# Scaling attention's projection weights on GpSimd ahead of its block sums, in a two-layer decoder step

## The reference, cut to what matters

```python
def rms_norm(x, gain):
    xf = x.astype(jnp.float32)
    xf = xf * lax.rsqrt(jnp.mean(xf * xf, axis=-1, keepdims=True) + RMS_EPS)
    return (xf * gain.astype(jnp.float32)).astype(x.dtype)

def shared_kv(h, norm_kv, w_kv, k_norm, w_fgate, b_fgate):
    u = rms_norm(h, norm_kv)
    k, v = jnp.split(u @ w_kv, 2, axis=-1)
    ...
def fox_layer(x, norm_g, w_in, q_norm, w_o, k_all, v_all, c_all):
    q, gate = jnp.split(rms_norm(x, norm_g) @ w_in, 2, axis=-1)
    q = rms_norm(q.reshape(bsz, t, B_HEADS, B_DH), q_norm)
    o = forgetting_attention(q, k_all, v_all, c_all)
    o = o.reshape(bsz, t, B_WIDTH).astype(x.dtype) * jax.nn.silu(gate)
    return x + o @ w_o, ...
```

## Time and profile before

| | |
|---|---|
| median of 3 runs | 1575.26 us |
| lowest and highest run | 1572.15 and 1576.94 us |
| span of the profiled execution, first to last instruction | 1572.7 us |
| mean granted TensorE clock | 0.995 |
| TensorE busy | 1529.1 us, 97% |
| VectorE busy | 1010.7 us, 64% |
| ScalarE busy | 713.1 us, 45% |
| GpSimd busy | 434.0 us, 28% |
| multiplications by the norms' factors, L457, on VectorE | 32, 1.22 us each |
| GpSimd's idle time ahead of the key multiplications, L845 | 226.5 us |
| GpSimd's idle time ahead of the first block sum, L708 | 257.0 us |

### The profile page before, as it was taken

The page is one execution under the profiler, slowest core; times in us unless marked ns, Lnnn a source line. Parts: engine busy times, 40 slices in busy tenths (PEclk is TensorE's granted clock), DMA queues, the critical chain, the costliest instruction groups (busy, mean ns, idle before and its releaser), DMA issues.

```text
span 1572.7 us, 23771 instructions
## 1 busy us (share of the span) xinstructions
PE 1529.1 (97%) x8705; PEld 1135.8 (72%) x8705; DVE 1010.7 (64%) x1979; ACT 713.1 (45%) x1412; POOL 434.0 (28%) x336
## 2 busy tenths in 40 slices
PE   6999999999999999999999999999999999998997
PEld 4688888888888874446777777777777777764543
DVE  7478696877869684135465776767676767676311
ACT  4344455544445552121365555555465555545100
POOL 6012222121222101012243425343343425332200
PEclk9999999999999999999999999999999999999999
DMA  9663929466482943223233545364444445475231
GB/s 267 175 191 120 265 73 269 123 188 194 130 246 89 271 174 84 78 87 100 82 95 107 161 161 175 135 199 137 156 137 142 157 161 175 148 235 216 89 131 42
DMA packets 254085, 242.32 MB, mean 154 GB/s; under 512 B 23162, under 2 KB 219962, under 8 KB 253970
## 3 DMA queue, kind: packets, MB, share of 16 engines
q1 hardware_dynamic: 242834, 204.21, 42.5%
q0 software_dynamic: 11136, 36.59, 6.6%
HBM read 212.63 MB, written 95.24 MB: 196 GB/s over the span
## 4 chain that ended last, share of the span: by engine, by line
PE 90%; DVE 5%; ACT 3%; issue 2%; DMA 0%; SPq 0%; POOL 0%; DVEq 0%; ACTq 0%; POOLq 0%
PE psum L1987 46%; PE psum L2011 7%; PE psum L2496 7%; PE psum L2294 5%; PE psum L2317 4%; PE psum L2301 3%; PE psum L2064 3%; PE psum L2256 2%; PE psum L2350 2%; PE psum L1975 2%; PE psum L2134 1%; PE psum L2150 1%; PE psum L2075 1%; PE psum L2162 1%; PE psum L2152 1%
## 5 line engine op out<-in xcount | busy, mean ns | idle before, releaser
L1987 PE MATMUL psum<-arena 128*128 128x252 f32 (+1 forms) x3472 | 815.2, 385 | 4.5 <-ACT arena L921 3.9
L1987 PEld LDWEIGHTS psum<-arena 128*128 128x128 f32 x3472 | 643.1, 191 | 125.8 <-issue 30.5
L1339 DVE TENSOR_TENSOR arena<-arena,psum 128x252 f32<-128x252 f32 (+1 forms) x310 | 130.6, 421 | 205.0 <-PE psum L1987 195.9
L845 POOL TENSOR_TENSOR arena<-arena 128x1024 f32<-128x1024 f32 x64 | 160.7, 2511 | 226.5 <-DMA arena<-k_pages 208.6
L1157 ACT ACTIVATE arena<-psum,arena 128x256 f32<-128x256 f32 (+7 forms) x128 | 93.7, 739 | 117.0 <-DVE arena L1684 116.7
L921 ACT COPY arena<-psum 128x252 f32<-128x252 f32 (+1 forms) x124 | 45.9, 370 | 172.3 <-PE psum L1987 172.2
L2496 PE MATMUL psum<-arena 128*128 128x512 f32 x256 | 114.4, 597 | 0.0
L2011 PE MATMUL psum<-arena 128*128 128x512 f32 x256 | 113.1, 594 | 0.1
L708 POOL TENSOR_TENSOR arena<-arena 128x512 f32<-128x512 f32 x31 | 40.9, 1319 | 257.0 <-issue 127.0
L1166 ACT ACTIVATE arena<-arena 128x256 f32<-128x256 f32 (+7 forms) x128 | 92.4, 770 | 2.1
L2011 PEld LDWEIGHTS psum<-arena 128*128 128x128 f32 x256 | 47.5, 190 | 57.5 <-issue 56.5
(11 more groups left out here) (265 smaller groups left out, 2150.8 us busy)
## 6 DMA issues: line engine op xcount, KB each, us to landing
k_pages<-in_cache_k SPq DMA_DIRECT2D x64, 512.0 KB, 6.5
v_pages<-in_cache_v SPq DMA_DIRECT2D x64, 512.0 KB, 7.2
arena<-k_pages SPq DMA_DIRECT2D x64, 512.0 KB, 3.6
arena<-v_pages SPq DMA_DIRECT2D x64, 512.0 KB, 5.7
arena<-in_w_in_a SPq DMA_DIRECT2D x32, 512.0 KB, 6.9
arena<-in_x_prompt SPq DMA_DIRECT2D x16, 512.0 KB, 5.5
arena<-in_w_kv SPq DMA_DIRECT2D x16, 512.0 KB, 5.6
arena<-in_w_in_b SPq DMA_DIRECT2D x16, 512.0 KB, 7.3
```

The source lines that it names most:

```text
L845: pool.tensor_tensor(k_ring[:, m % 2], k_ring[:, m % 2], q_all[:, m % S:m % S + 1, :].broadcast_to([P, PAGES, P]), ALU.mult).then_inc(kq_m ...
L1339: dve.tensor_tensor(out, more, bank[n % 2][:, 0:size(u)], ALU.add).then_inc(of.by_dve, 1)
L1987: ins = pe.matmul(bank[n % 2][:, 0:size(u)], w[:, k, :], x[:, k, :], start=(k == 0 and r in (0, 1, 3, 4)), stop=(k == HK - 1), skip_group_ ...
```

## The change

`scale_w` is issued by GpSimd instead of VectorE. Each call leaves its place in VectorE's list, and two calls stand at the head of `sums_of_kq` and of `sums_of_vg`. The waits for the loads move with them; GpSimd then waits for its own scalings before the sums. One wait is added, ahead of the first K and Q scaling, for the loads of the factors.

```diff
-        def scale_w(dve, w, gain, p, loaded, scaled):
-
-            dve.wait_ge(loaded, 16 * (p + 1))
-            dve.tensor_tensor(w, w, gain.unsqueeze(2).broadcast_to([P, KT, P]), ALU.mult).then_inc(scaled, 1)
+        def scale_w(pool, w, gain, p, loaded, scaled):
+
+            pool.wait_ge(loaded, 16 * (p + 1))
+            pool.tensor_tensor(w, w, gain.unsqueeze(2).broadcast_to([P, KT, P]), ALU.mult).then_inc(scaled, 1)
...
             def sums_of_kq(q):
+                scale_w(pool, w_k, gain_kv, q, w_k_loaded, w_k_scaled)
+                scale_w(pool, w_q, gain_b, q, w_q_loaded, w_q_scaled)
                 pool.wait_ge(w_k_scaled, q + 1)
                 pool.wait_ge(w_q_scaled, q + 1)
...
             def sums_of_vg(p):
+                scale_w(pool, w_v, gain_kv, p, w_v_loaded, w_v_scaled)
+                scale_w(pool, w_g, gain_b, p, w_g_loaded, w_g_scaled)
                 pool.wait_ge(w_v_scaled, p + 1)
                 pool.wait_ge(w_g_scaled, p + 1)
...
                 if s == TT - 3:
+                    pool.wait_ge(keys_in, 16 * 10)
                     sums_of_kq(0)
...
             me.chain(dve.tensor_scalar(gain_q2, gain_q2, -(DH ** -0.5), None, ALU.mult))
-            scale_w(dve, w_k, gain_kv, 0, w_k_loaded, w_k_scaled)
-            scale_w(dve, w_q, gain_b, 0, w_q_loaded, w_q_scaled)
             tile(5)
             tile(6)
-            scale_w(dve, w_v, gain_kv, 0, w_v_loaded, w_v_scaled)
-            scale_w(dve, w_g, gain_b, 0, w_g_loaded, w_g_scaled)
             tile(TT - 1)
...
             vg_add(0, 8)
-            scale_w(dve, w_k, gain_kv, 1, w_k_loaded, w_k_scaled)
             new_score(0)
...
                 vg_add(p, 10)
-                if p == 0:
-                    scale_w(dve, w_q, gain_b, 1, w_q_loaded, w_q_scaled)
                 row_max(p, 1)
...
                 kq(5)
-                if nxt:
-                    scale_w(dve, w_v, gain_kv, p + 1, w_v_loaded, w_v_scaled)
                 row_max(p, 4)
...
                 kq(8)
-                if nxt:
-                    scale_w(dve, w_g, gain_b, p + 1, w_g_loaded, w_g_scaled)
                 row_max(p, 5)
...
                 vg(3)
-                if p + 2 < PAIRS:
-                    scale_w(dve, w_k, gain_kv, p + 2, w_k_loaded, w_k_scaled)
                 row_max(p, 7)
...
                     new_score(p + 1)
-                if p + 2 < PAIRS:
-                    scale_w(dve, w_q, gain_b, p + 2, w_q_loaded, w_q_scaled)
```

## The result

| | before | after |
|---|---|---|
| median | 1574.65 us (4 runs, 1572.15 to 1576.94) | 1589.88 us (4 runs, 1584.28 to 1591.44) |
| ratio, 95% interval | | 1.0085 (1.0068 to 1.0101) |
| span of the profiled execution | 1572.7 us | 1589.7 us |
| mean granted TensorE clock | 0.995 | 0.995 |
| VectorE busy | 1010.7 us | 1012.1 us |

The kernel is 15.2 us slower, 17.0 us by the two spans. The forecast was 31.0 us slower with a range from 9 to 45: direction and range held, the size was twice too large.

The account below looks back on a forecast made before the run. TensorE bounds the kernel, so only its waits count; GpSimd's scalings would hold VectorE at the shared port. Terms 18.0 + 6.0 + 0.5 + 4.8 - 0.8 + 2.5 = 31.0 us slower gave 1606.3 us, range 1584 to 1620.

Parts of the forecast that it names:

- What bounds the kernel: TensorE is 90% of the span; the 39 us of multiplications VectorE loses are nearly all beside TensorE's work.
- Price of a scaling: Each GpSimd scaling over 128x1024 takes 2.36 us, as its key multiplication does: 4.7 us per pair of matrices, 76 us in all.
- Clock: Behind the 3.0 us V and gate waits the clock falls four times of six: 6.0 us, bounds 0 and 9.
- V and gate, the mechanism: Pairs 1 to 6: GpSimd's scalings hold shift and gate, delaying the softmax copy; TensorE waits 3.0 us each, 18.0 us.
- Rival (a): VectorE keeps the port for adjacent operations, gate right behind shift; TensorE waits 0.7 us per pair: 1586.5 us, chance 0.12.
- at each end the one that waits goes next: GpSimd and VectorE sharing the port: an operation holds the other engine to its own end, then the waiting one goes.
- K and Q, pairs' ends: Ends of pairs 0 to 5: block sums delay VectorE's norm; TensorE waits 0.8 us six times, 4.8 us, bounds 1.2 and 8.4.
- a coin's toss: At pairs' ends, norm first costs TensorE 0.2 us, second K and Q sum first 1.4 us; 0.8 taken.
- Before the pairs: V and gate scaling at 715 takes turns with VectorE's four differences, done about 728.7 instead of 726.1: 2.5 us, bounds 1 and 4.
- Start of pair 0: First row maximum comes earlier, gaining 2.7 us with the clock; TensorE waits 1.9 us for K and Q sums: -0.8 us.
- Pair 0's V and gate: No shift there; the gate, issued as the first scaling starts, waits one scaling, and slack takes most: 0.5 us.

Follow-up runs that it names:

- the last run: Kernel before, with pair 1's K scaling behind the second row maximum and pairs 1 to 7's V and gate scalings on GpSimd, a wait between them: ratio 0.9987.
- by-queries run: Changed kernel, with V and gate weights of pairs 1 to 7 multiplied by a row of the sample queries instead of the norm's factors: ratio 1.0134, 22.8 us slower.
- the run with the earlier scalings: Changed kernel, with each next pair's V and gate scalings one key multiplication earlier in GpSimd's list, block sums left in place: ratio 1.0191.
- the V and gate run: Kernel before, with only the V and gate scalings moved to GpSimd, those of K and Q on VectorE: ratio 1.0056.
- the K and Q run: Kernel before, with only the K and Q scalings moved to GpSimd, those of V and gate on VectorE: ratio 0.9999.

## Why the prediction was right in direction and wrong in size

**What bounds the kernel: right.** 39 us taken off VectorE gained nothing by themselves here, nor did 17 us in the last run.

**Price of a scaling: wrong, and the main error.** The step that failed was "I take it for the new ones", 2.36 us. It measured 1.89 us. The two scalings of a pair end 0.95 us earlier, and TensorE, itself ready 0.25 us later than I had it, waits 1.8 us on average instead of 3.0. Term: 18.0 forecast, 10.7 measured; with 2.36 us it is 16.3 (by-queries run). The nearest row had the same shape, 128x1024, but another kind of second operand: a full row of other numbers, repeated, where the scaling has one number for each block of 128. The block sums, two full operands, agree with the key multiplication (1.27 us for 512 columns). As to the rule of the Trainium skill ("GPSIMD Engine Reference", section "Engine selection") that such work is about twice as slow on GpSimd: against 1.22 us on VectorE the ratio here is 1.55, and 1.93 only with the full operand.

**Clock: the term falls with the price.** 6.0 us forecast for four falls of six; one fall, 1.7 us, came. In the by-queries run, with waits of the predicted size, three of six. The second fall of the changed kernel's trace, at 1555.67, belongs to a wait that both kernels have. The prediction read from the page's clock digits that no fall followed this wait before; the digits cannot show it, since they stay at 9 across the fall at 775 too. The trace's own clock does: it is 1.00 from 1536 to 1545 us, so the reading was right.

**V and gate, the mechanism: right here, by a rule that does not hold everywhere.** The order of events was as written: shift held, second scaling next, gate behind it. Rival (a), in which VectorE keeps the port, would have shown 1.2 us in the gate's row; it shows 2.93. At both boundaries the one that was waiting went next: the shift at the end of the first scaling, then the second scaling, which stands issued from 1077.32 on, then the gate. Where GpSimd still waits for a semaphore at that moment, nothing of it is waiting, and VectorE goes on with two adjacent operations, as in rival (a). The prediction wrote this condition down ("whose second scaling is then waiting") without seeing what a wait between the two would be worth. And "at each end the one that waits goes next" is too strong as a rule: in the run with the earlier scalings it failed at ten boundaries.

**K and Q, pairs' ends: too large, by the price and by a wait.** 4.8 forecast, 2.7 measured. I called it a coin's toss whether the norm or the second sum goes first. Timelines of GpSimd, VectorE and TensorE at an end of a pair in the changed kernel, which answer to the earlier trace rows:

```profile
1119.25 1.28 POOL L709 TENSOR_TENSOR arena<-arena 128x512 f32<-128x512 f32 x1
1120.05 1.56 DVE L1651 SCALAR_TENSOR_TENSOR arena<-arena 128x1032 f32<-128x1032 f32 x1
1120.61 2.15 POOL L710 TENSOR_TENSOR arena<-arena 128x512 f32<-128x512 f32 x1
...
1123.41 0.71 DVE L1764 TENSOR_SCALAR arena<-arena 8x8 f32<-8x8 f32 x1
...
1124.27 0.35 PE L2322 MATMUL psum<-arena 8*128 8x8 f32 x2 [0.45 <-DVE arena L1764]
```

The scalings being shorter, the norm L1651 comes in the midst of the second sum, L709, and not at the change from the first to the second. The third sum, L710, waits for a semaphore, so the norm went first in all six pairs. No toss: 0.39 to 0.51 us each.

**Before the pairs: too large, by the price again.** 2.5 forecast, 1.2 measured (from 0.6 us ahead to 0.55 behind; the V and gate run loses 1.2 there as well, the K and Q run nothing). GpSimd and VectorE there, which answer to the earlier trace rows:

```profile
714.29 4.31 POOL L457 TENSOR_TENSOR arena<-arena 128x1024 f32<-128x1024 f32 x2
...
718.70 7.94 DVE L1570 TENSOR_TENSOR arena<-arena 128x1056 f32<-128x1056 f32 x4 [1.29 <-ACT arena L1066]
718.73 2.35 POOL L708 TENSOR_TENSOR arena<-arena 128x512 f32<-128x512 f32 x1
```

The scalings are over at 718.6, before the four differences begin, so these take turns with the four sums alone and are done at 726.6, not 728.7. I had counted one scaling among them, again by the price of 2.36 us.

**Start of pair 0: right, the gain a little small.** Forecast: 2.7 gained and 1.9 lost, -0.8. Measured: 1.14 us of waiting and 1.7 us of clock gained, 1.07 us lost for the sums, which two scalings of 1.89 us delay less: -1.8. Pair 0's V and gate (0.5) cost nothing that shows.

**Sum.** 18.0 + 6.0 + 0.5 + 4.8 - 0.8 + 2.5 = 31.0 against 10.7 + 1.7 + 0 + 2.7 - 1.8 + 1.2 = 14.5, plus 1.7 for the fall at the end and 1.4 in the last pair and small gaps, less the 0.6 up to 720 us, 17.0. Of the 16.5 us between 31.0 and 14.5, 11.6 hang on V and gate and their clock, that is on one duration.

## What to carry to other kernels

Moving work to GpSimd is priced by what it holds up on VectorE, and there by the length of each single operation and by whether the next is already issued when it ends, not by the total: one wait moved between two GpSimd operations gave back ten us, and in another place two gave back 25. It is no rule for every place: ahead of the pairs the same wait cost 1.1 us. Take the duration of an operation from a row with the same kind of operands, not only the same shape. Before putting work on GpSimd beside a chain that TensorE waits for, list all of VectorE's instructions there, the smallest too: a 0.2 us operation was the one that cost most.
